# Laying 32 experts on three weight buffers: another sort of the experts, another order of filling the buffers

## The reference

```python
grp = jnp.argmax(group_logits, axis=-1)
in_group = expert_logits[jnp.arange(T), grp]
top_val, top_idx = lax.top_k(in_group, TOP_K)
expert_id = grp[:, None] * EXPERTS_PER_GROUP + top_idx
...
def expert_block(args):
    xb, e = args
    a = xb @ w_gate[e]
    u = xb @ w_up[e]
    return (jax.nn.silu(a) * u) @ w_down[e]
```

## Time and profile before

| | us |
|---|---|
| median of 3 runs | 2004.18 |
| the runs | 2002.65 to 2008.54 |
| the profiled execution | 2005.99 |
| its span in the trace | 2004.4 |
| last stretch: bookkeeping | 1458 to 1484 |
| expert loop, first to last `gate_up` start | 1484.4 to 1965.0 |
| close | 1965.0 to 2004.4 |

### The profile page before, as it was taken

How to read it: one execution, slowest core, us unless ns; L and a number is a source line. 1 busy time by engine, 2 the same in 40 slices (tenths; PEclk the granted TensorE clock), 3 DMA queues, 4 the chain that set the end, 5 groups by cost and what they waited for, 6 DMA issues and landing times.

```text
span 2004.4 us, 27790 instructions
## 1 busy us (share of the span) xinstructions
PE 1830.3 (91%) x9844; PEld 1282.7 (64%) x9844; DVE 852.8 (43%) x1321; ACT 441.9 (22%) x813; POOL 1043.6 (52%) x643
## 2 busy tenths in 40 slices
PE   7999999999999899999999889998968978869787
PEld 6888888887776678888888656765743323323232
DVE  6444434320444577444444489876341111111114
ACT  3111100100344432111100144552321111111112
POOL 7888887777544378888887533321212222212220
PEclk9999999999999999999999989999979989989887
DMA  4333342432211133333333212211588999999996
GB/s 161 94 94 98 112 176 96 146 95 89 63 60 43 43 95 91 98 94 94 96 110 101 74 53 74 64 52 31 205 313 345 388 399 398 397 409 400 411 385 215
DMA packets 54339, 338.87 MB, mean 169 GB/s; under 512 B 8266, under 2 KB 8650, under 8 KB 42256
## 3 DMA queue, kind: packets, MB, share of 16 engines
q1 hardware_dynamic: 45216, 317.21, 43.7%
q0 software_dynamic: 6288, 12.81, 2.1%
q10 hardware_dynamic: 2784, 8.19, 1.2%
HBM read 475.06 MB, written 15.09 MB: 245 GB/s over the span
## 4 chain that ended last, share of the span: by engine, by line
PE 71%; DMA 14%; DVE 10%; ACT 3%; issue 1%; POOL 1%; SPq 0%; DVEq 0%; ACTq 0%; POOLq 0%
PE bank L486 31%; DMA big<-w_up_in 13%; PE bank L457 12%; PE bank L1882 7%; PE bank L740 4%; PE bank L1366 4%; DVE big L1092 2%; PE bank L505 2%; PE bank L1900 2%; PE bank L1480 2%; PE bank L1908 1%; PE bank L658 1%; DVE state L1077 1%; PE bank L718 1%; PE bank L2092 1%
## 5 line engine op out<-in xcount | busy, mean ns | idle before, releaser
L299 POOL TENSOR_TENSOR weights_hi_parts<-ring,ones 128x1024 fp32r<-128x1024 f32 (+1 forms) x174 | 352.0, 2023 | 280.4 <-PE bank L486 120.1
L301 POOL TENSOR_TENSOR ring_parts<-ring,weights_hi_parts 128x1024 fp32r<-128x1024 f32 (+1 forms) x174 | 468.3, 2691 | 13.7
L486 PE MATMUL bank<-attention_buffers_parts,weights_hi_parts 128*128 128x512 f32 x832 | 325.9, 392 | 11.6 <-POOL small L235 10.2
L486 PE MATMUL bank<-state_parts,weights_hi_parts 128*128 128x512 f32 x832 | 324.4, 390 | 0.0
L486 PE MATMUL bank<-attention_buffers_parts,ring_parts 128*128 128x512 f32 x832 | 324.4, 390 | 0.0
L1882 PE MATMUL bank<-big,work 128*32 128x512 f32 x1440 | 223.5, 667 | 57.4 <-DMA big<-w_up_in 57.4
L457 PE MATMUL bank<-big_parts,weights_hi_parts 128*128 128x512 f32 x704 | 217.0, 389 | 1.2 <-POOL ring_parts L301 1.2
L912 POOL TENSOR_TENSOR ring_parts<-ring,weights_hi_parts 128x1024 fp32r<-128x1024 f32 x32 | 80.6, 2519 | 225.8 <-ACT weights_hi_parts L909 225.8
L486 PEld LDWEIGHTS bank<-attention_buffers_parts,weights_hi_parts 128*128 128x128 f32 x832 | 156.7, 188 | 45.4 <-POOL small L235 10.2
L486 PEld LDWEIGHTS bank<-state_parts,weights_hi_parts 128*128 128x128 f32 x832 | 156.8, 188 | 32.9 <-issue 0.5
L486 PEld LDWEIGHTS bank<-attention_buffers_parts,ring_parts 128*128 128x128 f32 x832 | 156.6, 188 | 32.5
(11 more groups left out here) (418 smaller groups left out, 2930.8 us busy)
## 6 DMA issues: line engine op xcount, KB each, us to landing
big<-w_up_in SPq DMA_DIRECT2D x54, 2048.0 KB
ring<-wdense_in SPq DMA_DIRECT2D x176, 512.0 KB, 3.6
state<-w_down_in SPq DMA_DIRECT2D x37, 2048.0 KB
big<-w_gate_in SPq DMA_DIRECT2D x36, 2048.0 KB
attention_buffers<-w_gate_in SPq DMA_DIRECT2D x18, 2048.0 KB
ring<-w_down_in SPq DMA_DIRECT2D x18, 2048.0 KB
ring<-wff_in SPq DMA_DIRECT2D x32, 704.0 KB, 4.1
results_by_token<-big ACTq DMA_DIRECT2D x1, 4096.0 KB, 15.5
```

What stands on the lines that cost most here:

```text
L299: po.tensor_tensor(hi, raw, ones[:, 0:1].to_broadcast([128, words]), ALU.mult).then_inc(PO.sem, 1)
L301: po.tensor_tensor(lo, raw, hi.bitcast(F32), ALU.subtract) \
L486: m = pe.matmul(out, x, y_, start=j + n == 0, stop=j == len(pairs) - 1 and n == len(ts) - 1)
```

## The change

The sign of the sort key now depends on the expert's number: odd experts are sorted from many blocks to few and come first, even ones follow from few to many. (`ways` holds +64 for odd and -64 for even numbers.) Stream 1 is filled first (behind expert 1), then stream 2, then stream 0; steps without a block come at the end of stream 0. For that, every place is moved by one: `quota` of the first three experts is -1, 0, 1, and 1 is added at the end.

```diff
-    DV.step(dv.tensor_copy(quota[:, 0:3], iota_f[:, 0:3]))
-    nb, numbers = sm(33), sm(33)
+    DV.step(dv.tensor_scalar(quota[:, 0:3], iota_f[:, 0:3], -1.0, None, ALU.add))
+    nb, numbers, ways = sm(33), sm(33), sm(33)
...
-    DV.step(dv.tensor_scalar(numbers[:, 32:33], tok_id[:, 0:1], float(NO_ROW), None, ALU.add))
+    DV.run(dv.tensor_scalar(numbers[:, 32:33], tok_id[:, 0:1], float(NO_ROW), None, ALU.add))
+    DV.run(dv.tensor_copy(ways.bitcast(I32), numbers))
+    DV.run(dv.tensor_scalar(ways.bitcast(I32), ways.bitcast(I32), 1, None, ALU.bitwise_and))
+    DV.run(dv.tensor_copy(ways, ways.bitcast(I32)))
+    DV.run(dv.tensor_scalar(ways, ways, 128.0, -64.0, ALU.mult, ALU.add))
...
-    DV.run(dv.scalar_tensor_tensor(key, nb, 64.0, numbers, ALU.mult, ALU.subtract))
+    key = ways
+    DV.run(dv.tensor_tensor(key, nb, ways, ALU.mult))
+    DV.run(dv.tensor_tensor(key, key, numbers, ALU.subtract))
...
-    DV.run(dv.tensor_scalar(shift, heads[:, 1:3], float(SETS), 1.0, ALU.mult, ALU.add))
+    DV.step(dv.tensor_scalar(shift[:, 0:1], heads[:, 2:3], float(SETS), 1.0, ALU.mult, ALU.add))
+    DV.run(dv.tensor_scalar(shift[:, 1:2], heads[:, 0:1], float(SETS), -2.0, ALU.mult, ALU.add))
...
-    DV.step(dv.tensor_scalar(quota[:, 3:32], banks[1][:, 259:288], heads[:, 0:1], float(SETS), ALU.add, ALU.mult))
+    DV.step(dv.tensor_scalar(quota[:, 3:32], banks[1][:, 259:288], heads[:, 1:2], float(SETS), ALU.add, ALU.mult))
...
-    DV.step(dv.tensor_scalar(unfilled, turn, total, float(SETS), ALU.subtract, ALU.mult))
...
-    DV.step(dv.tensor_tensor(shift[:, 1:2], shift[:, 1:2], unfilled, ALU.add))
...
-    DV.run(dv.tensor_tensor(place, place, late, ALU.add))
+    DV.run(dv.scalar_tensor_tensor(place, place, 1.0, late, ALU.add, ALU.add))
```

More of the change, by code:

```diff
@@ L1674, in build @@
     ranked = PE.step(m)
-    heads, ids1, key, ahead = sm(3), sm(C2), sm(33), sm(1)
+    heads, ids1, ahead = sm(3), sm(C2), sm(1)
     pair, total, most, rest, all_but_two, turn = sm(1), sm(1), sm(1), sm(1), sm(1), sm(1)
-    shift, past, unfilled = sm(2), sm(1), sm(1)
+    shift, past = sm(2), sm(1)
     more, spread = work[0:32, 2992:2992 + 29], work[0:32, 2960:2992]
```

## The result

The changed kernel was **slower by 0.25%**: ratio 1.0025, 95% interval 1.0014 to 1.0037, or +5.0 us (+2.8 to +7.4). The medians of 8 runs each were 2010.18 and 2003.98 us. Repeated on two other chips beside later experiments it gave 1.0013 (1.0003 to 1.0024) and 1.0021 (1.0010 to 1.0032). Taken together that is about +4 us. The direction was forecast and the time lies in the stated range; the size was not: +10.3 was forecast. Its profiled execution took 2007.56 us, the shortest of its eight, with a span of 2006.0.

What follows compares the result with a forecast made beforehand. The prediction took the expert loop, a race of weight queue and TensorE, as the bound. Loop +14.8, bookkeeping +1.0 and close -5.5 made +10.3 us on 2004.18, so 2014.5 us; range 2007.5 to 2019.5.

Steps and rivals of the forecast that it cites:

- What bounds the kernel: Expert loop: a race of the queue delivering weight matrices and TensorE at 7.07 us a step; neither rules alone.
- the 1936 that I had named as a sign of being wrong: Expert loop: the forecast is wrong if step 48 starts by 1936; it was expected near 1943.
- Counting the queue: Expert loop: weight matrices numbered in queue order, 86 in both layouts, at 5.53 us each, to time their landings.
- Number 82: Expert loop, changed layout: the up matrix of step 48, the 82nd in the queue, taken to land at 1942.0.
- The two readings: Landing of step 48's up matrix: 1943.6 with 5.53 us a matrix and 3 us idle, 1940.5 with 5.50 and 2.6.
- the walk: Both step tables followed at 7.07 us a step and 5.53 a matrix: queue empty 9.4 us before, 2.6 now.
- The bookkeeping: VectorE's routing operations ahead of the first step: extra operations delay everything after them by +1.0 us, bounds 0.6 and 1.3.
- The close: From step 53's start to the end: earlier scatter and adds remove TensorE's pause; -5.5 us, bounds -1.5 and -9.5.
- this case: Close: TensorE does not pause, sums run at 0.25 us each, giving 9.5 in place of 5.5; 2010.5 us, 12%.
- The bytes rival: Expert loop: bound by bytes, so less queue idle brings all 4 us earlier; -8.5 us in sum, 1995.7 us, 4%.
- The dense-queue rival: Expert loop: the queue delivers faster where dense, 5.45 us a matrix, 6 us less; 2008.5 us, 12%.

Runs made afterwards that it cites:

- both queues late: Changed kernel with GpSimd's last transfers and SyncE's loads of the first results held until step 53's `gate_up` ends; 1.0065 against before, +8.8 us against the changed kernel.
- the three other kernels with a pause: Changed kernel with GpSimd's and SyncE's transfers held back (1.0065); kernel before with only the new sort key (0.9997); kernel before with streams filled 1, 0, 2 (1.0070).
- both that move the empty step: Kernel before with its step without a block moved from step 5 to 53 (0.9994); changed kernel with its own moved from step 51 to 3 (0.9968 against before).
- streams 2, 0, 1: Kernel before with stream 2 filled first, then 0, then 1, and the step without a block at step 4; 0.9962, -7.6 us.
- the one with the sum first: Kernel before with the last block's sum put ahead of the adds in VectorE's queue, layout untouched; 0.9982, -3.6 us.
- both improvements together: Kernel before with streams filled 2, 0, 1 and the last block's sum ahead of the adds in VectorE's queue; 0.9966, -6.8 us.
- the layouts with an early empty step: Changed kernel with its step without a block at step 3 (-6.4 us against before); kernel before with streams filled 2, 0, 1, that step at 4 (-7.6 us).
- the changed kernel with its empty step early: Changed kernel with the step without a block moved from stream 0's last step (51) to its second lap (3); 0.9968 against before, -6.4 us.

## Why the prediction was right in its direction and wrong in its size

**What bounds the kernel: right.** Steps 5 and 6 wait, step 6 44.0 us behind step 3 (forecast 44), step 48 waits, 50 does not, and from step 49 on the four steps to 53 are 7.07 us apart. Step 48 began at 1937.5 in this trace, near the 1936 that I had named as a sign of being wrong; the next paragraph says why.

**Counting the queue: right in its make, 3.0 us too much.** Number 82 came 430.1 us after step 3. The two readings said 434.7 and 431.6, and I took the mean, 433.1; the second was nearer. The idle was 2.0 us (share 0.95 over 40 us; the later dips are left in the price of a matrix, as they are for the kernel before), and (430.1 - 2.0) / 78 = 5.49 us a matrix, not 5.53. Whether before's queue idled for 7.0 us (by the shares of one window) or 9.4 (by the walk) no run settles. From step 48 to 53 it took 38.2, forecast 37.8. Together +12.2 for +14.8.

**The bookkeeping: right**, +1.0 for +1.0.

**The close: this step failed.** Its term was mis-sized, -9.1 where -5.5 was taken, with -9.5 as its bound. Up to the last sum each time came nearly as worked out: adds issued at -2.5 (forecast -1.5), first landing +7.6 (+8.1), last sum ended +10.7 (+10.7). One sum in it has a slip: a scatter issued at -5.9 that lands 2.6 us later is there at -3.3 and not at -2.2, and the adds did go out 1 us sooner than forecast; it cost nothing, since the last sum waited for ScalarE. What failed is what I made of the clock. I had seen the sums at the low level for 15.7 us, and that they had run at the high level ahead of the pause, and took for the forecast that nearly all would be slow even without a pause. They were fast. In these runs the level in the close goes by the pause ahead of the sums: with 4.6 us before and 5.0 with both queues late it fell, with 0.6 it did not. I named this case as a rival, gave it 12%, and put it at 2010.5. That rival's mechanism is what happened; that its time is within 0.3 us of the measured median of 2010.18 is luck. It kept +14.8 for the loop, which took 2.6 us less, and the terms as the traces show them, +4.1 on a median of 2003.98, would give 2008.1.

The sentence that set the Trainium skill's rule (TensorE: Matmul & The Clock Gate, "What's actually happening": activity releases the throttle) against the trace drew too much from one row. That these products do not release the throttle is shown again, by the three other kernels with a pause (15.73, 15.73 and 15.18 us). That they would not hold it was my own addition, and six kernels without a pause show that they do hold it (the changed one, both that move the empty step, streams 2, 0, 1, the one with the sum first, and both improvements together: 44 records in 9.71 us each).

**The rivals.** The bytes rival (1995.7) was wrong for the reason given: three steps without a load cannot be hidden. Its -8.5 us is near what the layouts with an early empty step reach (-6.4 and -7.6), but they have both: a full queue and a late last load. The dense-queue rival was right by half of its size: it put 5.45 us for a matrix where the forecast put 5.53, and 5.49 came.

**What stays open.** Changed against before lies between +2.6 and +5.0 us by three comparisons, the profiles say +3.5 to +4.1; what makes the difference between the three is not settled, nor why the changed kernel with its empty step early gained 4 us more in the loop than its theory gave.

## What to carry to other kernels

Where a load queue and an engine race, walk the table of steps with the two prices: the order of the same work moved this kernel by 22 us from best to worst, with the same bytes. Spread new loads so that the queue never runs out, put empty steps where the queue is behind and not at the end, and let the last load be wanted one or two steps before the end. And ahead of a closing stretch of small products look for a pause: the products behind it may run at the low clock. What its removal is worth depends on what else is late: here TensorE was done 12.6 us sooner and the close was 4.7 us shorter.

## What was not expected of the hardware

TensorE's clock in the close went by the pause ahead of the sums, though it was busy without a break in them: with pauses of 3.6, 3.9, 4.6 and 5.0 us the 36 sums took 15.2 to 15.7 us at 0.50 (but for the first 0.6 us of the 15.2), with none or 0.6 us they ran at 1.00 (8.0 us for 36). In the loop the level fell too when TensorE waited for an up matrix, but there it came back while `gate_up` ran: in the kernel before 0.67 in 1520 to 1525 and 1.00 from 1525 on, with a `gate_up` of 5.1 us in place of 3.6. GpSimd's four adding transfers took 9.4 to 10.8 us to the first landing beside SyncE's four loads, and 5.4 us when those were nearly through, so that holding GpSimd's queue back by 6.8 us lengthened the close by 1.3 us in the profile.
